# Weights of two tiles woven element by element, in a split-float32 transformer kernel

## What is computed

```
h = rms_norm(x, g)
u = h @ w_in ; ... ; y = gelu(scan(u)) ; val, gate = split(y @ w_glu) ; x += val * sigmoid(gate)
x = x + ffn(rms_norm(x))            # 4 of them: up (1024 x 5632), gate, down (2816 x 1024)
x = x + sigmoid(rms_norm(x) @ w_gate) * (p @ w_proj)
k, v, q = projections ; x += attention(q, k, v) @ w_o       # three kinds of attention
```

## Time and profile before

| | |
|---|---|
| median of 3 runs | 1310.63 us (1309.89 to 1311.55) |
| the profiled execution, its own time | 1310.93 us |
| its span, first to last instruction | 1309.2 us |
| PE matmuls, PE weight loads, each | 10976 |
| busy: PE, PEld | 1278.9 us, 1228.8 us |
| busy: POOL | 1003.9 us |
| busy: ACT, DVE | 681.7 us, 641.3 us |
| HBM read | 213.26 MB |

### The profile page before, as it was taken

One profiled execution on the slowest core, in us unless ns is written; L12 is line 12 of the kernel. 1 busy time (PEld: TensorE's weight loads), 2 busy tenths in 40 slices (PEclk: granted clock), 3 DMA queues, 4 the chain that ended last, 5 costly groups with the idle time before them and its releaser, 6 DMA issues.

```text
span 1309.2 us, 27666 instructions
## 1 busy us (share of the span) xinstructions
PE 1278.9 (98%) x10976; PEld 1228.8 (94%) x10976; DVE 641.3 (49%) x1163; ACT 681.7 (52%) x944; POOL 1003.9 (77%) x793
## 2 busy tenths in 40 slices
PE   6999999999999999999999999999999999999999
PEld 5889999999989889999999878999999999999998
DVE  8995575555555748555555575211113454411112
ACT  7725544444676756434446565544346666644442
POOL 1226998889677659988887794988987766989985
PEclk9999999999999999999999999999999999999999
DMA  6304675555534334555554532555554433555530
GB/s 272 130 34 163 183 260 182 176 187 192 189 135 166 125 130 170 193 179 177 189 193 142 203 134 82 199 181 190 192 185 153 165 116 130 193 193 190 185 138 33
DMA packets 33879, 217.07 MB, mean 166 GB/s; under 512 B 3683, under 2 KB 7428, under 8 KB 8196
## 3 DMA queue, kind: packets, MB, share of 16 engines
q1 hardware_dynamic: 30096, 211.14, 45.5%
q10 hardware_dynamic: 3700, 4.75, 1.5%
HBM read 213.26 MB, written 2.62 MB: 165 GB/s over the span
## 4 chain that ended last, share of the span: by engine, by line
PE 83%; DVE 8%; ACT 5%; issue 2%; POOL 1%; DMA 0%; DVEq 0%; SPq 0%; ACTq 0%; POOLq 0%
PE up L1576 18%; PE up L1578 17%; PE up L1577 17%; PE acc L1576 7%; PE acc L1578 6%; PE acc L1577 6%; PE up L1711 2%; DVE opnd L980 2%; PE side L1803 2%; ACT w_hi L511 1%; PE acc L1769 1%; ACT opnd L649 1%; PE side L1584 1%; DVE mix L985 1%; PE up L1842 1%
## 5 line engine op out<-in xcount | busy, mean ns | idle before, releaser
L421 POOL TENSOR_TENSOR w_lo<-ring,w_hi 128x512 fp32r<-128x512 f32 x748 | 953.4, 1309 | 222.3 <-ACT w_hi L511 219.2
L1576 PE MATMUL up<-opnd,w_hi 128*128 128x256 f32 x2064 | 588.2, 285 | 4.1 <-DVE opnd L980 1.6
L1577 PE MATMUL up<-opnd,w_lo 128*128 128x256 f32 x2064 | 578.5, 280 | 0.0
L1578 PE MATMUL up<-opnd,w_hi 128*128 128x256 f32 x2064 | 578.1, 280 | 0.0
L511 ACT ACTIVATE w_hi<-ring 128x2048 fp32r<-128x2048 f32 x188 | 359.4, 1913 | 250.1 <-PE up L1578 191.2
L1576 PEld LDWEIGHTS up<-opnd,w_hi 128*128 128x128 f32 x2064 | 388.5, 188 | 16.6 <-issue 13.8
L1577 PEld LDWEIGHTS up<-opnd,w_lo 128*128 128x128 f32 x2064 | 390.2, 189 | 1.3 <-issue 1.0
L1578 PEld LDWEIGHTS up<-opnd,w_hi 128*128 128x128 f32 x2064 | 388.9, 188 | 0.0
L1576 PE MATMUL acc<-opnd,w_hi 128*128 128x256 f32 x784 | 221.7, 283 | 1.4 <-DVE x L1226 1.2
L1578 PE MATMUL acc<-opnd,w_hi 128*128 128x256 f32 x784 | 220.6, 281 | 0.0
L1577 PE MATMUL acc<-opnd,w_lo 128*128 128x256 f32 x784 | 219.7, 280 | 0.0
(11 more groups left out here) (296 smaller groups left out, 1424.4 us busy)
## 6 DMA issues: line engine op xcount, KB each, us to landing
ring<-in_stream SPq DMA_DIRECT2D x197, 1024.0 KB, 4.8
bias_rows<-mix ACTq DMA_DIRECT2D x1, 1536.0 KB
mix<-in_s_b SPq DMA_DIRECT2D x1, 1024.0 KB, 6.3
x<-in_x SPq DMA_DIRECT2D x1, 1024.0 KB, 8.3
mix<-in_s_c SPq DMA_DIRECT2D x1, 1024.0 KB, 12.3
mix<-bias_rows ACTq DMA_DIRECT2D x1, 1024.0 KB, 5.7
out_x<-x SPq DMA_DIRECT2D x8, 128.0 KB, 1.7
mix<-in_p ACTq DMA_DIRECT2D x2, 256.0 KB, 3.5
```

Source lines behind the costliest of these rows:

```text
L421: ins = nc.gpsimd.tensor_tensor(w_l[:, cols], ring[:, r, cols], w_h[:, cols].bitcast(f32), ALU.subtract)
L1576: MM(o, l_hi, r_hi, start=start, stop=False, skip_group_check=True)
L1577: MM(o, l_lo, r_hi, start=False, stop=False, skip_group_check=True)
L1578: return MM(o, l_hi, r_lo, start=False, stop=stop, skip_group_check=True)
```

## The change

In `w_hi` and `w_lo` the two tiles of each pair are interleaved: where 128 elements of tile m = 0 were followed by 128 of tile m = 1, now element q of tile 0 and element q of tile 1 are neighbours. The ring and the stream stay as they are. ScalarE, GpSimd and VectorE read the ring in the old order (`landed`) and write, and read `w_hi`, with a step of two elements (`woven`). A weight load of a tile reads 128 elements with a step of two (`tile`). In token slots the moving operand takes one tile and then the other, each with a step of two (`tiles`). Numbers, sizes and the order of instructions are the same on every engine. GpSimd's four pieces are now tile m of one half of the slot instead of quarters in a row.

```diff
+        def landed(v):
+            return v.rearrange("p (g m q) -> p m g q", m=2, q=P)
+        def woven(v):
+            return v.rearrange("p (g q m) -> p m g q", m=2, q=P)
+        def tile(v, g, m):
+            return woven(v)[:, m, g]
+        def tiles(v, g):
+            return woven(v)[:, :, g]
...
                 for q in range(QUARTERS):
-                    cols = slice(q * 2048 // QUARTERS, (q + 1) * 2048 // QUARTERS)
-                    ins = nc.gpsimd.tensor_tensor(w_l[:, cols], ring[:, r, cols], w_h[:, cols].bitcast(f32),
-                                                  ALU.subtract)
+                    m, g = q % 2, slice(4 * (q // 2), 4 * (q // 2) + 4)
+                    ins = nc.gpsimd.tensor_tensor(woven(w_l)[:, m, g], landed(ring[:, r])[:, m, g],
+                                                  woven(w_h.bitcast(f32))[:, m, g], ALU.subtract)
                 c.up(ins, "w_ready")
...
-                c.up(A(weights_hi(s), ring[:, s % RING], ACT.Copy), "w_hi_ready")
+                c.up(A(woven(weights_hi(s)), landed(ring[:, s % RING]), ACT.Copy), "w_hi_ready")
...
-                c.up(TTo(w_lo[s % SPLIT], ring[:, s % RING], w_hi[s % SPLIT].bitcast(f32), ALU.subtract), "w_ready")
+                c.up(TTo(woven(w_lo[s % SPLIT]), landed(ring[:, s % RING]), woven(w_hi[s % SPLIT].bitcast(f32)),
+                         ALU.subtract), "w_ready")
...
                     for m in range(2):
-                        w = slice((2 * k + m) * P, (2 * k + m + 1) * P)
-                        ins = three(o[:, m], w_h[:, w], w_l[:, w], hi(name)[:, k], lo(name)[:, k],
+                        ins = three(o[:, m], tile(w_h, k, m), tile(w_l, k, m), hi(name)[:, k], lo(name)[:, k],
                                     k == order[0] and m == 0, k == order[-1])
...
                     for t in range(TT):
-                        w = slice(2 * k * P, (2 * k + 2) * P)
                         q = slice(t * P, (t + 1) * P)
-                        ins = three(o[:, t], hi(name)[:, k, q], lo(name)[:, k, q], w_hi[b][:, w], w_lo[b][:, w],
+                        ins = three(features(o[:, t]), hi(name)[:, k, q], lo(name)[:, k, q], tiles(w_hi[b], k),
+                                    tiles(w_lo[b], k),
                                     k == 0 and t == 0, k == KT - 1)
...
-                b, w = s % SPLIT, slice((8 * k + m) * P, (8 * k + m + 1) * P)
-                return three(acc[:, m // 2, (m % 2) * T:(m % 2) * T + T], w_hi[b][:, w], w_lo[b][:, w],
+                w_h, w_l = (tile(v[s % SPLIT], 4 * k + m // 2, m % 2) for v in (w_hi, w_lo))
+                return three(acc[:, m // 2, (m % 2) * T:(m % 2) * T + T], w_h, w_l,
```

More of the change, by code:

```diff
@@ L1572, in bank, with features @@
                 return up[u % 2]
+            def features(v):
+                return v.rearrange("p (m q) -> p m q", m=2)
             def three(o, l_hi, l_lo, r_hi, r_lo, start, stop):
@@ L1897, in ple @@
                     for k in range(KT):
-                        w = slice((2 * k + m) * P, (2 * k + m + 1) * P)
-                        ins = three(banks[m], w_hi[s % SPLIT][:, w], w_lo[s % SPLIT][:, w], hi(name)[:, k], lo(name)[:, k],
-                                    k == 0, k == KT - 1)
+                        ins = three(banks[m], tile(w_hi[s % SPLIT], k, m), tile(w_lo[s % SPLIT], k, m), hi(name)[:, k],
+                                    lo(name)[:, k], k == 0, k == KT - 1)
                     c.up(ins, ("ple_half", "mm_done")[m])
@@ L1920, in diff_half @@
                         if kind == "v":
-                            w, q = slice(2 * k * P, (2 * k + 2) * P), slice(m * P, (m + 1) * P)
-                            ins = three(o[:, m], hi(name)[:, k, q], lo(name)[:, k, q], w_hi[b][:, w], w_lo[b][:, w],
+                            q = slice(m * P, (m + 1) * P)
+                            ins = three(features(o[:, m]), hi(name)[:, k, q], lo(name)[:, k, q], tiles(w_hi[b], k),
+                                        tiles(w_lo[b], k),
                                         first, last)
                         else:
-                            w = slice((2 * k + m) * P, (2 * k + m + 1) * P)
-                            ins = three(o[:, m], w_hi[b][:, w], w_lo[b][:, w], hi(name)[:, k], lo(name)[:, k],
+                            ins = three(o[:, m], tile(w_hi[b], k, m), tile(w_lo[b], k, m), hi(name)[:, k], lo(name)[:, k],
                                         first, last)
@@ L2156, in stick_half @@
                         if token:
-                            w = slice(2 * k * P, (2 * k + 2) * P)
                             q = slice(m * P, (m + 1) * P)
-                            ins = three(o[:, m], hi("odd")[:, k, q], lo("odd")[:, k, q], w_hi[b][:, w], w_lo[b][:, w],
+                            ins = three(features(o[:, m]), hi("odd")[:, k, q], lo("odd")[:, k, q], tiles(w_hi[b], k),
+                                        tiles(w_lo[b], k),
                                         first, last)
                         else:
-                            w = slice((2 * k + m) * P, (2 * k + m + 1) * P)
-                            ins = three(o[:, m], w_hi[b][:, w], w_lo[b][:, w], hi("odd")[:, k], lo("odd")[:, k],
+                            ins = three(o[:, m], tile(w_hi[b], k, m), tile(w_lo[b], k, m), hi("odd")[:, k], lo("odd")[:, k],
                                         first, last)
```

## The result

The changed kernel takes **1374.9 us** (median of 4 runs, 1374.3 to 1375.6). The kernel before, run beside it, takes 1310.3. The ratio is 1.0489, with a 95% interval of 1.0475 to 1.0502: slower by 64.6 us. The forecast was 1261 and faster. The range held the time only because rivals on the other side were in it.

The account below looks back on a forecast made before the run. TensorE's matmul pitch of 117.5 ns, from meetings of load and moving stream, was taken as the bound. 1310.9 - 54 (feature slots) + 0 (token slots, ScalarE, VectorE) + 4 (GpSimd) = 1260.9, stated as 1261 us; 8-in-10 range 1243 to 1375.

Parts of the forecast that it names:

- The reading of the bound: TensorE's `three`: matmul pitch of 117.5 ns makes most of the time, as load and moving stream meet in memory.
- Rival 2: TensorE: pitch stays at 117.5 ns because meetings are not its cause; 1311 us, chance 0.13.
- the feature term: Feature slots on TensorE: step-two loads bring the pitch to 110.4 ns on 7,640 matmuls, saving 54 us.
- The token term: Token slots on TensorE: moving weights with a step of two costs 0, bounds up to 37 us.
- Rival 1: Token slots on TensorE: loads gain, but moving weights run at half speed, giving back 37 us; 1298 us, chance 0.07.
- the zeros: ScalarE, GpSimd and VectorE: reading or writing with a step of two was taken to cost 0.
- rival 3: GpSimd becomes the bound through slower low parts, 1390 us at 25% longer, 1640 us at 1.6 times; chance 0.15.
- The named covers: ScalarE's 191 us of waits for matmuls, and GpSimd's 5.05 us against TensorE's 5.64 us per slot, hide slower work.
- the 0 to 13 that stood for ScalarE: ScalarE's high part: step-two writes cost 0, at most 13 us, the high parts not hidden on the chain.
- The 4 us for late GpSimd pieces: GpSimd at stage openings: it catches up more slowly, three to four late pieces of 1.26 us, between 0 and 13.
- Rival 4: TensorE feature loads: meetings double, the 8.1 ns excess doubles on 7,640 loads; 1373 us, chance 0.13 including the extreme.
- Its extreme: TensorE feature loads: a load runs at half its rate, 216 ns pitch, 753 us more; 2064 us, chance 0.03.

Follow-up runs that it names:

- experiment 7: Kernel before without the four pads between weight buffers and before operands, loads with neighbours: 1326.8 us.
- experiment 10: Kernel before with no pads except 64 bytes ahead of the first operand buffer, loads with neighbours: 1308.9 us.
- experiment 11: Kernel before with no pads except 128 bytes ahead of the first operand buffer, loads with neighbours: 1317.6 us.
- experiment 12: Kernel before with no pads except 192 bytes ahead of the first operand buffer, loads with neighbours, one run: 1278.3 us.
- experiment 16: Kernel before with no pads except 224 bytes ahead of the first operand buffer, loads with neighbours: 1315.9 us.
- experiment 4: Kernel before with feature-slot loads reading at a step of four, token slots and writes as before: 2322.5 us.
- experiment 8: Kernel before with feature-slot loads at a step of two and the pads removed, writes and token slots as before: 1327.2 us.
- experiment 14: Kernel before with feature-slot loads reading at a step of sixteen, token slots and writes as before: 2211.0 us.
- experiment 2: Changed kernel with TensorE reading neighbours again, while ScalarE, GpSimd and VectorE still write woven: 1314.2 us.
- experiment 5: Kernel before with the moving stream of the second matmul, L1577, cut from 256 to 128 columns: 1300.0 us against 1309.8.
- experiment 9: Kernel before with the weight load of L1577 cut from 128 to 64 columns: 1300.7 us against 1311.4.
- experiment 15: Kernel before with no pads except 192 bytes ahead of the first operand buffer, timed over several runs: 1281.2 us, ratio 0.9793.

## Why the prediction was wrong

**The reading of the bound was right.** The time is the pitch of `three`. How the buffers of the two streams of TensorE lie changes that pitch: experiments 7, 10 to 12 and 16 show 113.3 to 120.0 ns with only pads moved, and at one offset two paces exist, as the prediction's "on addresses and on the phase" allows. That the streams delay each other in the memory is the likely reason, and is argued. "TensorE: Matmul & The Clock Gate" of the Trainium skill (Part 2: What happens when you issue a matmul) has two independent read ports, one for each stream. If that meant that a load takes nothing from a running matmul and addresses don't matter, these runs disagree. Rival 2, the unchanged pitch, fell with the 119.9 ns.

**The step that failed is the feature term.** It said that with a step of two "both run side by side at equal speed, as in L1727", a pitch of 110.4 ns, worth 54 us. Measured: 119.9 ns, and a loss of 16.6 us. By the rows, 7,640 matmuls x (119.9 - 117.5) = 18 us. The mistake was to compare the streams in bytes passed. L1727 differs from `three` in more than that: it moves 128 columns where `three` moves 256, so it showed that a load with neighbours fits into 109.4 ns, and not that matched byte speeds do. Experiments 4, 8 and 14 show what a step costs a load: at two, the pitch of the worst offset, 120 ns, and at four and sixteen twice that. The sum took the step itself at nothing.

**The token term was taken at the wrong end.** I took 0, with bounds to 37 us, "since VectorE's step-two reads are free". It is 43.9 us. That was a row of another engine, moving 512 elements in 690 ns, which is 1.35 ns per element; TensorE moves one in 118 / 256 = 0.46 ns. A row at a third of the rate can't tell whether the fast reader has room. Its bound was too low as well: the pitch is 230 ns, where I had 216 from L1711, and nearly all 432 matmuls count, not 377. 432 x (230 - 118) = 48 us, of which 43.9 appear. Some of the rest is waits that are gone: the token group's idle 1.7 us is 0.0 now. Rival 1 named this mechanism, and it was given 0.07.

**ScalarE, GpSimd, VectorE: the zeros nearly held, by their covers.** The high part takes 2115 ns, 10% more, where the prediction read no cost from L631. It could have read one: L631's 399 ns are 25 more than the 374 of L670, whose source also lies in PSUM, and 25 ns on 256 elements would be 200 on 2048; 202 were measured. L628 at 417 ns reads SBUF, which hid it. The three lines differ in more than the step, so this is a hint and no proof. The low part is 5.15 us per slot instead of 5.05, from the timeline of POOL after:

```profile
200.43 5.15 POOL L437 TENSOR_TENSOR w_lo<-ring,w_hi 128x512 fp32r<-128x512 f32 x4 [0.60 <-ACT w_hi L527]
```

That is 2%, where rival 3 needed 12% to decide. The named covers held: all writes together cost 3.3 us (experiment 2), inside the 0 to 13 that stood for ScalarE. The 4 us for late GpSimd pieces were priced for a faster TensorE, and no run had that together with woven writes.

**Rival 4 gave 1373 us and the measurement 1374.9, and that is luck.** It had the sign of the feature slots right, and its "each piece of memory that it opens serves half as many elements" is close to the reading below; but its doubling would have put 125.6 ns into every feature slot. They have 119.9, a third of that loss, and the rest came from token slots, where it had nothing. A total that agrees proves no mechanism; the pitch of the two kinds of slot, read apart, did. Its extreme, a load at half its rate (216 ns), is what a step of four shows: 235 ns and 2322 us.

**A reading that fits these rows, argued and not shown.** Suppose each stream can open one piece of four neighbouring float32 elements every 1.74 to 1.84 ns, the 223 and 235 ns of experiments 14 and 4 over 128. A load of step one opens 32 pieces, one of step two 64 (111 to 118 ns: just fits), one of step four or sixteen 128. The moving stream opens 64 at step one (just fits) and 128 at step two (223 to 235 ns; measured 230). With pieces of two elements the load would have doubled at a step of two already, and with pieces of eight not yet at four. Pieces of this size stand in the Trainium skill, "SBUF — State Buffer", in the note on SBUF cachelines (under Door 1: The DMA port swizzle): 16-byte lines, and at least two hits on a line for the full rate. By that rule a step of two with float32 is free. For the load the trace agrees nearly (120 ns against 235 at four). For the moving stream it disagrees (230 against 118); that one reads twice as many elements in the time. By this reading step two turned the load, which had room, into a second stream without any, and turned the moving stream, which had none, into the bound. It remains open why 192 bytes is the best offset, why 224 loses nearly all of it, what chooses between two paces at one offset, whether finer offsets are better still, and why experiments 5 and 9 got back so little when either stream was cut.

## What to carry to other kernels

Keep neighbours in the operand that moves: a step of two almost doubled the pitch of 256-column matmuls (118 to 230 ns), while on the loaded operand it cost 2% (6% against the best offset) and a step of four doubled it. When a duration is borrowed from another engine, compare the rates per element first; a slow reader's zero says nothing of a fast one. Where the pitch of equal matmuls differs between slots, try the offset between the loaded and the moving buffers, in steps of 64 bytes or less, before reshaping any data: here other pads were worth 2.1%.

## What was not expected of the hardware

- Where a buffer lies in memory, and nothing else, moves a full kernel by 48 us (1278.3 to 1326.8 us, experiments 12 and 7).
- The same 48 matmuls on the same buffers take 5.44 us in one slot of the kernel before and 5.70 in another, without a gap and at full clock.
- The limit of a strided load doesn't grow with the step: 235 ns at four, 223 at sixteen, the larger step slightly the faster.
- A write with a step of two costs ScalarE 10% on 2048 elements (1913 to 2115 ns) and a write and read with it cost GpSimd 2% (1309 to 1336 ns).
- The runs of experiment 15 lie 7.9 us apart (1279.8 to 1287.7), those of the changed kernel 1.3. That fits a pitch with two paces at one offset, but no trace of a slower run of it was taken, so it isn't shown.
